# GpSimd's halves for more chunks of the mixer, and the norm's root behind its product

## What is computed

```python
for l in range(DEPTH):
    h = rmsnorm(x, norm_mix[l])
    (u_ssm, q_lat, kv_lat, k_rope, hg_q, hg_f, hg_i, hg_g, gate_logits) = jnp.split(h @ w_in[l], split_at, axis=-1)
    y_ssm = s5_mixer(u_ssm, ...)      # ends in gelu(y) @ ssm_w_glu[l], one half times sigmoid of the other
    y_mla = mla_mixer(q_lat, kv_lat, k_rope, ...)
    y_hg = hgrn2_mixer(hg_q, hg_f, hg_i, hg_g, ...)    # its last product is o @ hg_w_o[l]
    gates = jax.nn.sigmoid(gate_logits).reshape(bsz, s, 3, D_MODEL)
    x = x + (gates[:, :, 0] * y_ssm + gates[:, :, 1] * y_mla + gates[:, :, 2] * y_hg) @ w_out[l]
    x = x + memory_cross_attention(rmsnorm(x, norm_cross[l]), rmsnorm(mem, norm_mem[l]), ...)
    x = x + swiglu_ffn(rmsnorm(x, norm_ffn[l]), ffn_w_gate_up[l], ffn_w_down[l])
```

## Time and profile before

| | us |
|---|---|
| runs of the kernel before | 1942.86, 1946.78, 1950.49 (median 1946.78) |
| the profiled execution | 1944.08 |
| its span in the trace | 1942.2 |

### The profile page before, as it was taken

The page is one execution under the profiler, slowest core; times in us unless marked ns, Lnnn a source line. Parts: engine busy times, 40 slices in busy tenths (PEclk is TensorE's granted clock), DMA queues, the critical chain, the costliest instruction groups (busy, mean ns, idle before and its releaser), DMA issues.

```text
span 1942.2 us, 26797 instructions
## 1 busy us (share of the span) xinstructions
PE 1815.6 (93%) x9937; PEld 1424.7 (73%) x9937; DVE 1195.3 (62%) x1871; ACT 869.4 (45%) x1417; POOL 234.3 (12%) x243
## 2 busy tenths in 40 slices
PE   7999998989999999999888999998899999889998
PEld 6675656669998865666477998656799864669986
DVE  6995745545667892754554566655477745546775
ACT  4224445354444412344455445345555543555553
POOL 4004213020000001414012000111200000130000
PEclk9999999999999999999999999999999999899999
DMA  5444442445565444445154666531365654135553
GB/s 157 129 137 141 131 139 99 141 114 174 157 186 179 125 128 138 140 133 172 32 166 121 191 185 189 145 100 66 113 180 164 195 153 119 55 104 166 167 190 133
DMA packets 192358, 274.59 MB, mean 141 GB/s; under 512 B 25616, under 2 KB 129540, under 8 KB 192228
## 3 DMA queue, kind: packets, MB, share of 16 engines
q1 hardware_dynamic: 191364, 269.86, 45.7%
q0 software_dynamic: 864, 3.02, 0.5%
HBM read 271.78 MB, written 1.05 MB: 140 GB/s over the span
## 4 chain that ended last, share of the span: by engine, by line
PE 81%; DVE 8%; ACT 5%; issue 3%; POOL 2%; DMA 0%; DVEq 0%; ACTq 0%; POOLq 0%
PE bank L398 43%; PE bank L396 28%; DVE WL L1146 2%; ACT WH L1414 2%; PE bank L662 1%; PE bank L583 1%; POOL WL L1146 1%; PE bank L1006 1%; PE bank L591 1%; PE bank L856 1%; ACT HTH L1414 1%; PE bank L486 1%; DVE bank L2063 1%; PE bank L709 1%; PE bank L633 1%
## 5 line engine op out<-in xcount | busy, mean ns | idle before, releaser
L1146 DVE TENSOR_TENSOR WL<-W,WH 128x1024 fp32r<-128x1024 f32 x288 | 352.9, 1225 | 226.9 <-ACT WH L1414 218.6
L1414 ACT ACTIVATE WH<-W 128x1024 fp32r<-128x1024 f32 x328 | 347.5, 1060 | 323.1 <-PE bank L398 251.4
L398 PE MATMUL bank<-HTH,WH 128*128 128x256 f32 x1536 | 439.4, 286 | 24.6 <-DVE WL L1146 14.7
L398 PE MATMUL bank<-HTH,WL 128*128 128x256 f32 x1536 | 435.2, 283 | 0.0
L398 PE MATMUL bank<-HTL,WH 128*128 128x256 f32 x1536 | 435.2, 283 | 0.0
L398 PEld LDWEIGHTS bank<-HTH,WH 128*128 128x128 f32 x1536 | 295.3, 192 | 31.3 <-DVE WL L1146 17.8
L398 PEld LDWEIGHTS bank<-HTL,WH 128*128 128x128 f32 x1536 | 295.4, 192 | 0.5 <-issue 0.5
L398 PEld LDWEIGHTS bank<-HTH,WL 128*128 128x128 f32 x1536 | 295.3, 192 | 0.0
L398 PE MATMUL bank<-WH,HTL 128*128 128x512 f32 x544 | 216.8, 398 | 0.0
L398 PE MATMUL bank<-WH,HTH 128*128 128x512 f32 x480 | 196.0, 408 | 15.6 <-POOL WL L1146 9.4
L398 PE MATMUL bank<-WL,HTH 128*128 128x512 f32 x480 | 191.2, 398 | 0.0
(11 more groups left out here) (408 smaller groups left out, 2405.5 us busy)
## 6 DMA issues: line engine op xcount, KB each, us to landing
W<-in_w_in SPq DMA_DIRECT2D x132, 512.0 KB, 3.7
W<-in_ffn_w_gate_up SPq DMA_DIRECT2D x176, 256.0 KB, 3.4
W<-in_w_up SPq DMA_DIRECT2D x176, 256.0 KB, 3.5
W<-in_ffn_w_down SPq DMA_DIRECT2D x44, 512.0 KB, 4.2
W<-in_w_down SPq DMA_DIRECT2D x44, 512.0 KB, 4.3
W<-in_w_out SPq DMA_DIRECT2D x32, 512.0 KB, 4.0
W<-in_ssm_w_glu SPq DMA_DIRECT2D x16, 512.0 KB, 3.7
W<-in_x_w_kv SPq DMA_DIRECT2D x16, 512.0 KB, 3.8
```

The costliest lines, as they stand in the source:

```text
L398: m = pe.matmul(out, at_a(a[x]), at_b(b[y]), start=(start and i == 0), stop=(stop and i == 2), skip_group_check=True)
L1146: eng.tensor_tensor(WL[:, m % HSLOTS, 0:width], W[:, n % RSLOTS, 0:width], h, ALU.subtract)\
L1414: copy = lambda dst, src, scale=1.0: act.activation(dst, src, ACT.Copy, scale=scale)
```

## The change

1. The first two gates take "both" for every second chunk too. GpSimd splits only the four column tiles that these chunks use (2, 3, 6 and 7), once, right after the latent roots (`mix_halves`), and puts them into HTL.
2. The glu's four products of four column tiles take "both" for their second chunk each. GpSimd splits two tiles of UT (`glu_halves`).
3. All four chunks of `yh` are "both"; the transposed heads are split by ACT (high) and DVE (low, `low_of`), where ACT alone copied them.
4. GpSimd's order is now: the chunks of all gates, UT's halves, the glu's chunks, the load of the memory, the first chunk of `yh`, the memory norm's root, the other chunks.
5. The first mixer norm works as in layer 1: raw x is transposed, u is scaled on its way out of PSUM, and HTF is scaled by DVE (`mix_scaled`). The norm's gains have a load, a transpose and a bank of their own (`par0`); the other parameters come behind the first chunk. Part of GpSimd's constants is made later, and part of DVE's setup moves behind the scaling.
6. GpSimd's copy of the roots goes; `token_row` reads RSTD broadcast, and in the feed-forward layers it is issued after the last chunk of the first pair of columns, one chunk earlier.

```diff
             def token_row(n):
-                pe.wait_ge(sem["rstd_rows"], rows_at[n])
+                pe.wait_ge(sem["rstd"], n + 1)
                 ps = begin("rb", n)
                 for tt in range(TT):
-                    m = pe.matmul(ps[:, tt * P:tt * P + P], RSR[:, tt, :], IDENT[:, :], start=(tt == 0),
+                    m = pe.matmul(ps[:, tt * P:tt * P + P], RSTD[:, n, tt:tt + 1].broadcast_to([P, P]), IDENT[:, :], start=(tt == 0),
...
                 if l == 0:
-                    norm_T(nrm)
+                    pe.wait_ge(sem["x_rows"], 16)
+                    for j in range(4):
+                        raw_T(nrm, j, None)
...
-                ssm_u(0, 1)
                 if l:
-                    token_row(mix_norm)
+                    ssm_u(0, 1)
+                else:
+                    ssm_u(0)
+                    parameters()
+                    ssm_u(1)
+                token_row(mix_norm)
                 ssm_u(2)
...
+                pe.wait_ge(sem["mix_halves"], l + 1)
                 for n in range(2):
                     if l == 0 and n == 1:
                         ssm_out(l, 3)
-                    token_out(("gate", l, n), "w_in", l, HTF, KT, 3360 + 512 * n, 512, low=None)
+                    token_out(("gate", l, n), "w_in", l, HTF, KT, 3360 + 512 * n, 512, low=None, halves=mix_half)
                 level(l, 0)
-                pe.wait_ge(sem["gate_in"], l + 1)
                 for n in range(2, 6):
-                    token_out(("gate", l, n), "w_in", l, HTF, KT, 3360 + 512 * n, 512, low=None, halves=(GTH, HTL))
+                    token_out(("gate", l, n), "w_in", l, HTF, KT, 3360 + 512 * n, 512, low=None, halves=mix_half)
...
                 def glu(h):
-                    token_out(("glu", l, h, 1), "ssm_w_glu", l, UT, 4, DM + h * 512, 512, low=None)
-                    token_out(("glu", l, h, 0), "ssm_w_glu", l, UT, 4, h * 512, 512, low=None)
+                    token_out(("glu", l, h, 1), "ssm_w_glu", l, UT, 4, DM + h * 512, 512, low=None, halves=glu_half)
+                    token_out(("glu", l, h, 0), "ssm_w_glu", l, UT, 4, h * 512, 512, low=None, halves=glu_half)
...
-                token_out_wide(("yh", l), "hg_w_o", l, oHG, 4, low=None)
+                token_out_wide(("yh", l), "hg_w_o", l, oHG, 4, low="both")
...
-                            if (j, k0) == (1, 0):
+                            if (j, k0) == (0, KT - 2):
                                 token_row(n)
...
             for n, (name, srcs, k, cols) in enumerate(chunks):
+                if n == 1:
+                    first_params()
                 if n == RSLOTS:
                     later_params()
-                    sp.wait_ge(sem["consts"], 1)
+                    sp.wait_ge(sem["consts"], 2)
                     ssm_rows(0)
...
                 signal(last, "rstd", n + 1)
-                if n in rows_at:
-                    signal(pool.tensor_copy(RSR, RSTD[:, n, :].rearrange("p (t o) -> p t o", o=1)
-                                            .broadcast_to([P, TT, P])), "rstd_rows", rows_at[n])
...
+            def halves_of(dst, src, *ks):
+                pair = lambda t, k: t[:, k:k + 2, :].rearrange("p a b -> p (a b)")
+                for k in ks:
+                    high, low = pair(dst[0], half_slot(k)), pair(dst[1], half_slot(k))
+                    link(pool.tensor_copy(high, pair(src, k)))
+                    ins = pool.tensor_tensor(low, pair(src, k), high.bitcast(F32), ALU.subtract)
...
-                wait_full(pool, ("y", l, 3))
-                for k in range(2):
-                    part = lambda t: t[:, 4 * k:4 * k + 4, :].rearrange("p a b -> p (a b)")
-                    link(pool.tensor_copy(part(GTH), part(HTF)))
-                    ins = pool.tensor_tensor(part(HTL), part(HTF), part(GTH).bitcast(F32), ALU.subtract)
-                signal(ins, "gate_in", l + 1)
-                for m in range(split_before["gate", l, 1, 1], split_before["gate", l, 5, 1]):
-                    split_whole(m)
+                signal(halves_of(mix_half, HTF, 2, 6), "mix_halves", l + 1)
+                split_to(split_before["gate", l, 5, 1])
+                pool.wait_ge(sem["y_ready"], 4 * (l + 1))
+                signal(halves_of(glu_half, UT, 2), "glu_halves", l + 1)
+                split_to(split_before["glu", l, 1, 0, 1])
                 wait_full(pool, ("ho", l, 1))
                 load_mem()
+                split_to(split_before["glu", l, 1, 0, 1] + 1)
                 norm_rstd(nrm, halves=False)
                 nrm += 1
                 split_to(split_before["cv", l, 1])
...
                 for j in range(2):
-                    evict(two(oHG, j), "hoT", l, j)
+                    high_of(2 * j, 2, "hoT", l, j, dst=oHG[0])
...
                 glu_out(1)
                 norm_rows(nrm, memX, memX)
+                for j in range(2):
+                    low_of(2 * j, 2, "hoT", l, j, dst=oHG)
                 norm_cols(nrm, "norm_mem", l)
```

More of the change, by code:

```diff
@@ L478, in raw_T @@
             def raw_T(n, j, tag):
-                for tt in range(TT):
+                for tt in range(TT) if tag else ():
                     freed(*tag, tt, j // 2)
@@ L1299, in _, with both_parts @@
             lows = [0]
-            def split_to(m):
-                low_parts(pool, "pool", lows, m)
-            def split_whole(m):
-                n, who = splits[m]
-                assert who == "both"
+            def both_parts(m):
+                n, _ = splits[m]
                 width = chunks[n][2] * chunks[n][3]
@@ L1317, in split_whole, with split_to @@
                 signal(pool.tensor_tensor(low, raw, high.bitcast(F32), ALU.subtract), s, v)
-                lows[0] = m + 1
+            def split_to(upto):
+                for m in range(lows[0], min(upto, len(splits))):
+                    if splits[m][1] == "both":
+                        both_parts(m)
+                        lows[0] = m + 1
+                    else:
+                        low_parts(pool, "pool", lows, m + 1)
+            def halves_of(dst, src, *ks):
[4 more added lines that the diff above has]
+                    ins = pool.tensor_tensor(low, pair(src, k), high.bitcast(F32), ALU.subtract)
+                    if k != ks[-1]:
+                        link(ins)
+                return ins
             def load_mem():
@@ L1685, in _ @@
                     take_bu(l, 1)
-                else:
-                    for q in range(4):
-                        take_u(q)
                 if l == 0:
@@ L2314, in _, with take_u @@
             for l in range(DEPTH):
+                def take_u(q):
+                    wait_full(dve, ("u", l, q))
+                    free_after(tt_(UT[:, q, :], bank(("u", l, q))[:, 0:S], RB, ALU.mult), "u", l, q)
+                mix_gain = lambda k: gain("norm_mix", l, k, KT)
                 if l == 0:
[L2316 to L2317 removed]
+                    wait_freed(dve, ("par0",))
+                    for j in (1, 3):
+                        whole_cols(nrm, HTLF, mix_gain, j)
@@ L2339, in _ @@
-                    take_u(3)
+                    add_whole(nrm, HTLF, mix_gain, ("ffd", l - 1), RSTD[:, nrm - 1, :])
+                for _ in phases(l, 2 if l else 0):
+                    pass
+                wait_freed(dve, ("rb", nrm))
+                take_u(0)
+                take_u(1)
+                for _ in phases(l, 3 if l else 1):
+                    pass
+                take_u(2)
+                for j in range(0, KT // 2, 2):
+                    wait_freed(dve, ("hT", nrm, j))
@@ L2340, in _ @@
+                for k in range(0, KT, 4):
+                    ins = tt_(HTF[:, k:k + 4, :], HTLF[:, k:k + 4, :],
+                              RB.rearrange("p (o t) -> p o t", o=1).broadcast_to([P, 4, S]), ALU.mult)
+                signal(ins, "mix_scaled", l + 1)
+                take_u(3)
+                if l == 0:
+                    setup_steps()
                 nrm += 1
```

168 lines of the change are left out of this document (84 added, 84 removed).

## The result

The changed kernel takes 1923.88 us (median of 4 runs, 1920.52 to 1925.15), the kernel before 1946.11 (4 runs). The ratio is 0.988, with a 95% interval from 0.9863 to 0.9897: **22.2 us faster by the medians**, where 12.5 were forecast. The time lies inside the range that was given, close to its lower end; the size of the gain doesn't hold. The profiled execution has a span of 1922.6 us against 1942.2.

The account below looks back on a forecast made before the run. PE was taken as four fifths of the chain that bounds the kernel. Terms 5.6 + 2.8 - 2.6 + 0.5 + 0.4 + 5.8 = 12.5 us took the median from 1946.8 to 1934.3, range 1923 to 1943.

Parts of the forecast that it names:

- the start: First layer's start: a shorter wait for BT, set against a lower PE clock, gains +0.5 us, bounds -1.5 and +1.2.
- that load is set by SP's queue, not by PE: At the start, `ssm_b` waits for the last state row, 30.88 us, which reordering SP's loads would not bring earlier.
- the stage before `yh`: `glu(1)` and `yh`: 8.4 us saved by halves, 11.0 waited as GpSimd's splits hold DVE; loses 2.6 in all.
- row in the feed-forward layers: Row one chunk earlier removes PE holes: 3.4 us in the first block and 2.4 in the second.
- halves in gates 0, 1 and the glu: Chunks in halves save 0.70 us each: 5.6 us in the gates, 2.8 in `glu(0)`, and more in `glu(1)`.
- What would show it: Profile signs: 12 products of 2.73 us; wrong if PE waits at L662, L1984 stays 0.5 or block two's second hole goes.
- rivals 3 and 4: Slower: DVE's level chain falls behind, 1961 us, chance 0.06; GpSimd late with the glu's halves, 1948 us, chance 0.08.
- Rival 2: Feed-forward layers: the earlier row gives nothing, as PE waits at the next chunk instead; 1940 us, chance 0.16.
- the layer-1 row: Layer 1: the wait for GpSimd's copy of the roots, 0.36 us, goes; a gain of +0.4 us.
- the clock term: At the start, a PE hole of 5 us should bring the lower 1.2 GHz level to `ssm_b` as well.
- whether L1984 passes or is held: Memory norm's scaling on DVE: taken to wait for GpSimd's subtraction; if not, the stage gains 1.7 us a layer.
- Rival 1: Before `yh`, GpSimd and DVE don't collide as forecast; 1923 to 1928 us, chance 0.27.

Follow-up runs that it names:

- start_alone: Changed kernel with gates 0 and 1, glu and level heads' product plain and the feed-forward row late; 2.8 us below the kernel before by the medians.
- start_row: start_alone with the row's product one chunk earlier in the four feed-forward layers; 10.3 us faster than start_alone by the means.
- row_late: Changed kernel with the row's product back behind the first chunk of the second pair in the feed-forward layers; median 9.0 us above after_again.
- yh_plain: Changed kernel with the level heads' product plain again, its heads copied by ACT alone and none of its chunks split by GpSimd; 1920.59 us.
- norm_alone: start_alone with the small parameter loads ahead of the first weight chunk again; by time it can't be told from the kernel before.
- start_order: Changed kernel with the 13 small parameter loads ahead of the first weight chunk again; 2.8 us slower by the means.
- yh_wait: Changed kernel with GpSimd waiting, before splitting yh's second and third chunks, until DVE has scaled the memory's second tile; 1921.16 us.
- wait_and_w_first: yh_wait with the small parameter loads behind the third chunk of weights; 3.4 us slower than yh_wait by the medians.
- after_again: The changed kernel run once more, unedited, with a second profile; ratio 0.9896 to the kernel before.

## Why the prediction was right in direction and short in size

The surplus of about 10 us has three main sources. Two terms of the sum were wrong: the start, at +0.5, rests on "that load is set by SP's queue, not by PE", and the stage before `yh` on 11.0 us of waits, of which 5.2 came. And TensorE's clock was priced at the start only and put at nothing elsewhere. Each part beside its forecast, in us, by the means of the times and by "full":

```
part                                  forecast    time    "full"
start and layer 1's row (0.5 + 0.4)      0.9       2.4      3.5     before -> start_alone
row in the feed-forward layers           5.8      10.3      5.9     start_alone -> start_row (row_late: 10.3 and 5.7)
halves in gates 0, 1 and the glu        11.2      13.9     12.3     start_row -> yh_plain
halves in yh (5.6 saved, 11.0 waited)   -5.4      -4.3     -0.9     yh_plain -> changed
sum                                     12.5      22.3     20.8
```

The difference of the two sums, 1.5 us, is half of the time at half clock that the changed kernel has less (74.8 and 71.9 us). The third part, and in part the fourth, compare kernels run in different sets, so their times are the less certain (errors of 1.4 and 1.0, and the sets themselves). By time the row carries the largest part of the surplus; in work and waits the stage before `yh` and the start do.

1. **Gates and glu: right in mechanism, 1.1 us low by "full".** 0.70 us a chunk and 11.1 us in the stages, no wait at L671 (before L662); where the rest comes from is open. "What would show it" counts 12 such products in the gates and the glu; by the sum's own terms they are 16. DVE's level chain keeps up; rivals 3 and 4 fall.
2. **The row: right in the waits, not in the time.** The hole of 1.7 goes in the first block, one of two goes in the second, and the other stays as named, 5.7 us where 5.8 were forecast. The 4.5 us of clock that went with them in two surroundings are a term that the forecast didn't have. Rival 2 falls. The 0.36 us of the earlier trace rows are gone too, but PE now waits 0.63 for DVE's HTF (L2383) before `hf`, so the layer-1 row gave nothing; that term was wrong.
3. **The start: the step that failed** is "that load is set by SP's queue, not by PE: SP issues the same loads in another order and waits for nothing on its way". It took the time of an issue as fixed. The last state row's issue ended at 28.52 us before and at 27.04 and 27.21 in the changed kernel, and `ssm_b` began at 28.80 and 29.12, not at 30.88. Here 1.8 to 2.1 us are won that I held for impossible. The order of the loads isn't all of it: with the old order the issue ends at 27.88 and 27.97, and `ssm_b` begins at 29.65 and 29.66 (norm_alone, start_order), 1.2 us earlier already. What gives these 1.2 is open. The wait for BT went from 1.81 to 1.01 and 0.50, as forecast in direction. PE's rows there, in the changed kernel:

```profile
28.80 1.09 PE L620 MATMUL bank<-IDENT,HQ 128*128 128x128 f32 x8 [4.14 <-DMA HK<-in_ssm_c_im]
29.73 0.37 PE L765 MATMUL bank<-IDENT,M 88*128 88x88 f32 x2
31.11 3.97 PE L642 MATMUL bank<-UT,BT 32*128 32x256 f32 x32 [1.01 <-ACT BT L1551]
35.01 1.89 PE L629 MATMUL bank<-IDENT,HK 128*128 128x128 f32 x8
```

   The hole of 4.14 (5 was forecast) brought the lower level for more of what follows, 6.8 us where it was 3.4: L629 takes 1.89 us where it took 1.09. So the clock term was right in sign, too.
4. **Before `yh`: the mechanism was right, its terms were not.** The forecast asked whether L1984 passes or is held. It is held: 3.63 us beside GpSimd, 1.01 with GpSimd idle (yh_plain) or waiting (yh_wait). In the first layer, on the forecast's own scale (`glu(1)` at 260.53, so 4.49 added), L2029 ends at 280.27 where 281.0 was written, and `yh` starts at 282.32 where 282.45 was. That looks exact and is partly luck: 1.94 of it is that the transposes ran at half clock, which the forecast had not. The **term that was mis-sized is 11.0 us of waits**. PE's holes beyond the 1.39 that stays in yh_plain are 3.27 us in the first layer and 1.96 in the second (hole of 3.35), 5.2 in sum. I worked one layer out and took it twice. In the second layer L2502 came 0.03 us ahead of GpSimd's cast and not 0.14 behind it, so the cast had to wait, and only L2029 was held. By time the stage lost 4.1 in the profiles and 4.3 by the means against yh_plain, near the 5.4 of the forecast. But this is luck: waits of half the size, and most of the rest is the lower level behind the holes, 6.8 us in the first layer and 3.4 in the second.
5. **Rival 1** (no or a lighter collision, 1923 to 1928) gives the time that was measured, though its reason does not hold: by time its 6 us for the stage were 1.1, and the others came from the row, the halves and the start.

Of my three "what would show it" signs for the sum being wrong, none came: PE didn't wait at L671, L2029 wasn't 0.5, the second hole in the second block stayed. None of them looked at the start, at the second layer alone or at the clock. Among the signs for the forecast one failed: the hole between the two halves of the transposes is 0.56 us and not about 2.5.

One reading in the forecast is a little off, without weight for the sum: 2.76 us is not the rest of GpSimd's subtraction plus 0.69 (that is 2.91). L2396 ends 0.54 after the subtraction, and L2502 in the changed kernel 0.55 after GpSimd's instruction.

**A faster version.** Both yh_plain and yh_wait beat the changed kernel: 1920.59 and 1921.16 us by the medians against 1924.63. By "full" yh_wait is the better by 0.9 (error 0.4), and by the medians they can't be told apart.

## What to carry to other kernels

When two engines hold each other up, work out the collision for each place where it occurs, from that place's own arrival times: here 0.14 us ahead or 0.03 behind decided who was held, and the holes were 3.3 and 2.0 us. Where two starts are that close, give the term both values. Don't take the issue time of a DMA queue as fixed when an order changes. Price the clock in every stage in which a hole of PE comes or goes, from rows at either level, and not only where it is in view. And compare kernels by span times granted clock beside their mean times: the product shows work and waits (5.9 and 5.7 us for the row in two surroundings), the time shows what is really gained (10.3 in both). Where the two part, as in wait_and_w_first, the time says what the kernel takes.

## What the runs showed of the hardware

- A DVE `tensor_scalar` on fp32 with one input in SBUF and its scalar in SBUF (128x512) is held by GpSimd's subtraction as two-input instructions are: 3.63 us for two beside it, 1.01 without. With both inputs in SBUF, DVE's instruction was held when GpSimd's cast had started 0.01 to 0.14 us before it (1.45 and 1.58 us instead of 0.69), and the cast was held when DVE's had started 0.01 to 0.04 us before (1.55 to 1.58 us instead of 1.04). The Trainium skill, SBUF — State Buffer, section Who interferes with whom, says for VectorE's two-port modes, which `tensor_scalar` can enter, that whoever issues first gets the shared pair of ports for the whole instruction and the other is fully blocked, and that issue order decides who blocks; the traces agree, in both directions.
- TensorE's lower level came with PE busy for 8.00 of 8.00 us in one execution and not in another of the same kernel. The time at half clock is 65 to 81 us in the means of kernels whose work differs by 1%. A hole of 4.1 us was followed by the lower level in both profiles of the changed kernel, one of 3.35 in its second layer as well; one of 1.4 us at the same place, in yh_plain and yh_wait, was not. The hole of 2.96 us at 499 us was followed by it in yh_wait and not, at 502 us, in after_again. Why the level falls at one such place and not at another, these runs don't settle.
- SP's issue of a 512 KB load took 0.42 us by itself, 1.0 us as one of four in a row (3.99 in all) and 0.75 as one of three (2.26).
